# A hybrid decoder step: gate-score levels of both token blocks in one product each, the second block's keys in reversed token order

## The reference, cut to what matters

```
z = forget logits; k_in = (1 - lb) * sigmoid(-z); qh = silu(query logits)
# S_t = diag(f_t) S_{t-1} + k_t^T v_t ;  o_t = S_t^T q_t, so for n >= m
A[n, m] = sum_d q[n, d] k[m, d] exp(b[n, d] - b[m, d])     # b = cumulative sum of log f
o[n]    = sum_m A[n, m] v[m]        S_end = sum_m (k[m] * exp(b_end - b[m]))^T v[m]
```

## Time and profile before

| | |
|---|---|
| median of 3 runs | 1856.31 us |
| the profiled execution's own time | 1854.89 us |
| its span, first to last instruction | 1853.1 us |
| PE busy | 1809.0 us (98%) |
| DVE busy | 1148.3 us (62%) |
| ACT busy | 777.4 us (42%) |
| POOL busy | 278.5 us (15%) |
| mean granted TensorE clock | 0.995 |

### The profile page before, as it was taken

One profiled execution on the slowest core, in us unless ns is written; L12 is line 12 of the kernel. 1 busy time (PEld: TensorE's weight loads), 2 busy tenths in 40 slices (PEclk: granted clock), 3 DMA queues, 4 the chain that ended last, 5 costly groups with the idle time before them and its releaser, 6 DMA issues.

```text
span 1853.1 us, 37457 instructions
## 1 busy us (share of the span) xinstructions
PE 1809.0 (98%) x14672; PEld 1789.6 (97%) x14672; DVE 1148.3 (62%) x1293; ACT 777.4 (42%) x894; POOL 278.5 (15%) x332
## 2 busy tenths in 40 slices
PE   5999999999999999999999999999999999999997
PEld 5999999999999999999999999999999999999996
DVE  8776877768777674555556665555555555545444
ACT  5444444444544453333334344443344334333332
POOL 4441624516235110000000000000000000000001
PEclk9999999999999999999999999999999999999998
DMA  7665646656467555555557655555655555555552
GB/s 230 191 203 171 195 139 194 203 174 195 139 191 209 174 165 178 180 181 177 175 168 229 187 177 181 177 176 178 181 177 176 179 180 176 182 181 179 175 180 102
DMA packets 387002, 333.86 MB, mean 180 GB/s; under 512 B 10240, under 2 KB 385024, under 8 KB 386816
## 3 DMA queue, kind: packets, MB, share of 16 engines
q1 hardware_dynamic: 368000, 318.87, 56.5%
q10 hardware_dynamic: 18944, 14.16, 2.6%
HBM read 316.67 MB, written 16.32 MB: 180 GB/s over the span
## 4 chain that ended last, share of the span: by engine, by line
PE 84%; DVE 6%; issue 3%; DMA 3%; ACT 1%; SPq 1%; POOL 0%; DVEq 0%; ACTq 0%
PE pA L1062 13%; PE pA L1063 13%; PE pA L1064 12%; PE pB L1063 11%; PE pB L1062 11%; PE pB L1064 11%; DMA raw<-in_w_in 3%; PE p L1062 3%; PE p L1063 3%; PE p L1064 3%; DVE lo L703 2%; PE p L1205 1%; DVE hg_scores L914 1%; PE p L1177 1%; SPq L358 1%
## 5 line engine op out<-in xcount | busy, mean ns | idle before, releaser
L703 DVE TENSOR_TENSOR lo<-raw,hi 128x1024 fp32r<-128x1024 f32 x568 | 724.2, 1280 | 575.7 <-ACT hi L407 569.7
L407 ACT CAST hi<-raw 128x1024 fp32r<-128x1024 f32 x568 | 595.6, 1049 | 847.8 <-PE pA L1064 355.9
L1062 PE MATMUL pA<-h_hi,hi 128*128 128x264 f32 x1728 | 500.4, 290 | 19.0 <-DVE lo L703 19.0
L1063 PE MATMUL pA<-h_lo,hi 128*128 128x264 f32 x1728 | 493.9, 286 | 0.0
L1064 PE MATMUL pA<-h_hi,lo 128*128 128x264 f32 x1728 | 493.4, 286 | 0.0
L1062 PE MATMUL pB<-h_hi,hi 128*128 128x264 f32 x1472 | 422.2, 287 | 0.0
L1063 PE MATMUL pB<-h_lo,hi 128*128 128x264 f32 x1472 | 418.8, 285 | 0.0
L1064 PE MATMUL pB<-h_hi,lo 128*128 128x264 f32 x1472 | 418.4, 284 | 0.0
L1062 PEld LDWEIGHTS pA<-h_hi,hi 128*128 128x128 f32 x1728 | 328.1, 190 | 22.7 <-issue 19.2
L1063 PEld LDWEIGHTS pA<-h_lo,hi 128*128 128x128 f32 x1728 | 327.5, 190 | 0.3
L1064 PEld LDWEIGHTS pA<-h_hi,lo 128*128 128x128 f32 x1728 | 327.3, 189 | 0.0
(11 more groups left out here) (250 smaller groups left out, 2486.2 us busy)
## 6 DMA issues: line engine op xcount, KB each, us to landing
raw<-in_w_in SPq DMA_DIRECT2D x224, 512.0 KB, 3.7
raw<-in_w_fin SPq DMA_DIRECT2D x176, 512.0 KB, 3.7
raw<-in_w_fout SPq DMA_DIRECT2D x88, 512.0 KB, 3.5
raw<-in_w_ret SPq DMA_DIRECT2D x32, 512.0 KB, 3.8
raw<-in_w_out SPq DMA_DIRECT2D x32, 512.0 KB, 4.1
S_ret<-in_s_ret SPq DMA_DIRECT2D x8, 1024.0 KB, 8.4
out_ret_s<-S_ret ACTq DMA_DIRECT2D x8, 1024.0 KB, 7.0
raw<-in_w_hg SPq DMA_DIRECT2D x16, 512.0 KB, 3.6
```

Source lines behind the costliest of these rows:

```text
L407: copy(hi[s][:], raw[s][:]).then_inc(hi_done, 1)
L703: tt(lo[s][:], raw[s][:], hi[s][:].bitcast(F32), ALU.subtract).then_inc(split_done, 1)
L1062: mm(outs[t], w_hi, a_hi[:, kt, :], start=(kt == 0), stop=False)
L1063: mm(outs[t], w_hi, a_lo[:, kt, :], start=False, stop=False)
```

## The change

The seven level products of block 1 go away. `k_lev[n]` now has 128 columns: in the lower halves stand block 0's keys as before, and in the columns that were zero stand block 1's keys in reversed token order (reversing the 128 tokens turns lower halves into upper ones). One product then holds, in its 128 rows, keys of both blocks, and the predicate masks pick for block 0's queries the one kind of row and for block 1's the other. All that meets block 1's scores as rows is therefore in reversed order too: the diagonal product takes `hkey_back`, the mask of the diagonal gets a reversed identity, block 1 of `kbar` is written reversed, and the values come from `hval_back`.

Per head it removes 7 products on PE, adds one `tensor_scalar` of 128 columns on DVE (`hkey_back`, step 3), one copy of 128 columns on ACT (`hval_back`, step 15) with a semaphore on which PE waits at step 16, and on POOL it splits 7 writes of `k_lev` and one of `kbar` into two each. At the start, 7 memsets on POOL go away and the constants grow from 3776 to 4352 columns.

```diff
-        k_lev = [alloc(heads, f"k_lev{i}", [P, NP]) for i in range(NLEV)]
+        k_lev = [alloc(heads, f"k_lev{i}", [P, P]) for i in range(NLEV)]
...
                         act.wait_ge(b_free, h * 2 + 3)
+                        copy(hval_back[:], hig[:, 0, P:NP][:, ::-1]).then_inc(hval_turned, 1)
                         fn(hg_sig[:], hig[:, 1, :], ACT.Sigmoid).then_inc(hg_sig_done, 1)
...
-            for i in range(NLEV):
-                nc.gpsimd.memset(k_lev[i][:], 0.0).then_inc(products, 1)
...
                     kl0, _ = halves(k_lev[i][:], s)
+                    kl1, _ = halves(k_lev[i][:, ::-1], s)
+                    n, shape = P // (2 * s), [P, NP // (2 * s), s]
...
-                    step(tt(kl0, k0, g0, ALU.mult))
+                    tt(kl0, k0[:, 0:n], g0[:, 0:n], ALU.mult).then_inc(products, 1)
+                    count[0] += 1
+                    step(tt(kl1, k0[:, n:], g0[:, n:], ALU.mult))
...
-                step(tt(kbar[:], hkey[:, 0:NP], run_g[:], ALU.mult))
+                tt(kbar[:, 0:P], hkey[:, 0:P], run_g[:, 0:P], ALU.mult).then_inc(products, 1)
+                count[0] += 1
+                step(tt(kbar[:, P:NP][:, ::-1], hkey[:, P:NP], run_g[:, P:NP], ALU.mult))
...
                         ts(hkey[:], z_nsig[:], omlb[:, bass.ds(h, 1)], None, ALU.mult).then_inc(forget_done, 1)
+                        ts(hkey_back[:], z_nsig[:, P:NP][:, ::-1], omlb[:, bass.ds(h, 1)], None, ALU.mult)
...
-                            msk = c_level[:, n:n + 1, :].rearrange("p a (b s) -> p a b s", s=s
-                                                                   ).broadcast_to([P, 2, 64 // s, s])
+                            msk = c_level[:, n].rearrange("p k (b s) -> p k b s", s=s)
...
                     pe.wait_ge(parts_done, h * 14 + 14)
-                    natural(p7[:, 0, 0:256], hig[:, 0, :], 128)
+                    pe.wait_ge(hval_turned, h + 1)
+                    natural(p7[:, 0, 0:256], hig[:, 0, :], 128, second=hval_back[:])
...
                     for n in range(NLEV):
-                        mm(p56[:, 0, 64 * n:64 * n + P], k_lev[n][:, 0:P], q_lev[n][:], start=True, stop=True)
-                    for n in reversed(range(NLEV)):
-                        last = mm(p56[:, 1, 64 * n:64 * n + P], k_lev[n][:, P:NP], q_lev[n][:], start=True, stop=True)
+                        last = mm(p56[:, n // 4, (n % 4) * P:(n % 4) * P + P], k_lev[n][:], q_lev[n][:],
+                                  start=True, stop=True)
                     last.then_inc(p56_full, 1)
```

More of the change, by code:

```diff
@@ L86 @@
 K_LEVEL = K_MASK + H * NP
-K_IDENT = K_LEVEL + NLEV * 64
-K_KDEC = K_IDENT + P
+K_IDENT = K_LEVEL + NLEV * P
+K_KDEC = K_IDENT + 2 * P
 K_GAMMA = K_KDEC + 2 * H
@@ L140, in build @@
         hkey = alloc(heads, "hkey", [P, T])
+        hkey_back = alloc(heads, "hkey_back", [P, P])
+        hval_back = alloc(heads, "hval_back", [P, P])
         hquery = alloc(heads, "hquery", [P, T])
@@ L227, in build @@
         c_ident = cst[:, K_IDENT:K_IDENT + P]
-        c_level = cst[:, K_LEVEL:K_LEVEL + NLEV * 64].bitcast(I32).rearrange("p (l j) -> p l j", l=NLEV)
+        c_level = cst[:, K_LEVEL:K_LEVEL + NLEV * P].bitcast(I32).rearrange("p (l b j) -> p l b j", l=NLEV, b=2)
+        c_diag = cst[:, K_IDENT:K_IDENT + 2 * P].rearrange("p (b n) -> p b n", b=2)
         c_kdec = cst[:, K_KDEC:K_KDEC + 2 * H].rearrange("p (b h) -> p b h", b=2)
@@ L271, in build @@
         hg_sig_done = sem("hg_sig_done")
+        hval_turned = sem("hval_turned")
         products = sem("products")
@@ L622, in _ @@
             pool.wait_ge(h_done, 4)
-            for i in range(NLEV):
-                nc.gpsimd.memset(k_lev[i][:], 0.0).then_inc(products, 1)
-            steps = 2 + 4 * NLEV + 4
+            steps = 2 + 5 * NLEV + 5
             def last_outputs(h):
@@ L637, in levels @@
             def levels(h):
-                count = [NLEV]
+                count = [0]
                 def step(ins):
@@ L659, in levels @@
                     kl0, _ = halves(k_lev[i][:], s)
-                    shape = [P, NP // (2 * s), s]
+                    kl1, _ = halves(k_lev[i][:, ::-1], s)
+                    n, shape = P // (2 * s), [P, NP // (2 * s), s]
                     if i:
@@ L670, in levels @@
                 step(tt(run_g[:, 0:P], run_g[:, 0:P], run_f[:, NP - 1:NP].broadcast_to([P, P]), ALU.mult))
-                step(tt(kbar[:], hkey[:, 0:NP], run_g[:], ALU.mult))
-                assert count[0] == NLEV + steps
+                tt(kbar[:, 0:P], hkey[:, 0:P], run_g[:, 0:P], ALU.mult).then_inc(products, 1)
+                count[0] += 1
+                step(tt(kbar[:, P:NP][:, ::-1], hkey[:, P:NP], run_g[:, P:NP], ALU.mult))
+                assert count[0] == steps
             levels(0)
@@ L783, in level_psum @@
             def level_psum(n):
-                return bass.AP(tensor=p56, offset=64 * n, ap=[[2 * 512, P], [512 + 64, 2], [1, 64]])
+                return p56[:, n // 4, (n % 4) * P:(n % 4) * P + P].rearrange("p (k j) -> p k j", k=2)
             def state_lo(out, state, state_hi_part, h, n):
@@ L897, in head @@
                         tt(hg_scores[:, 0:3:2, :], p4[:, 0, 0:256].rearrange("p (b n) -> p b n", b=2),
-                           c_ident.rearrange("p (a n) -> p a n", a=1).broadcast_to([P, 2, P]), ALU.mult
-                           ).then_inc(score_step, 1)
+                           c_diag, ALU.mult).then_inc(score_step, 1)
                         nc.vector.tensor_copy(v_rows[4 * NS:8 * NS, 0:HV], p4[4 * NS:8 * NS, 0, 384:512]
@@ L1077, in _, with natural @@
                 pe.sem_inc(free, 1)
-            steps = 2 + 4 * NLEV + 4
-            def natural(out, src, width):
+            steps = 2 + 5 * NLEV + 5
+            def natural(out, src, width, second=None):
                 for b in range(2):
-                    last = transpose(out[:, b * width:b * width + 128], src[:, b * P:b * P + P], c_ident)
+                    block = src[:, b * P:b * P + P] if second is None or b == 0 else second
+                    last = transpose(out[:, b * width:b * width + 128], block, c_ident)
                 return last
@@ L1158, in attend @@
                 elif i == 16:
-                    pe.wait_ge(products, h * steps + (NLEV + steps))
+                    pe.wait_ge(products, h * steps + steps)
                     pe.wait_ge(p7_free, h * N7 + (TI2 + 1))
                     pe.wait_ge(parts_done, h * 14 + 14)
-                    natural(p7[:, 0, 0:256], hig[:, 0, :], 128)
+                    pe.wait_ge(hval_turned, h + 1)
+                    natural(p7[:, 0, 0:256], hig[:, 0, :], 128, second=hval_back[:])
                     natural(p7[:, 0, 256:512], kbar[:], 128).then_inc(p7_full, 1)
@@ L1167, in attend @@
                     for b in range(2):
-                        mm(p4[:, 0, b * P:b * P + P], hkey[:, b * P:b * P + P], hquery[:, b * P:b * P + P],
-                           start=True, stop=True)
+                        mm(p4[:, 0, b * P:b * P + P], hkey_back[:] if b else hkey[:, 0:P],
+                           hquery[:, b * P:b * P + P], start=True, stop=True)
                     mm(p4[:, 0, 256:384], k_top[:], q_lev[NLEV][:], start=True, stop=True)
@@ L1318, in constants @@
         n_of = (j // s) * 2 * s + s + j % s
-        level.append((m // (2 * s) == n_of // (2 * s)) & (m % (2 * s) < s))
+        seen = (m // (2 * s) == n_of // (2 * s)) & (m % (2 * s) < s)
+        level += [seen, seen[::-1]]
     kdec = gamma[None, None, :] ** (NP - 1 - (np.arange(2)[None, :, None] * P + np.arange(P)[:, None, None]))
@@ L1323, in constants @@
     c[:, K_MASK:K_MASK + H * NP] = mask.transpose(1, 0, 2).reshape(P, H * NP)
-    c[:, K_LEVEL:K_LEVEL + NLEV * 64] = np.concatenate(level, axis=1)
-    c[:, K_IDENT:K_IDENT + P] = np.eye(P)
+    c[:, K_LEVEL:K_LEVEL + NLEV * P] = np.concatenate(level, axis=1)
+    c[:, K_IDENT:K_IDENT + 2 * P] = np.concatenate([np.eye(P), np.eye(P)[::-1]], axis=1)
     c[:, K_KDEC:K_KDEC + 2 * H] = kdec.reshape(P, 2 * H)
```

## The result

The changed kernel takes 1840.72 us (median of 4 runs, 1839.6 to 1842.7) against 1856.38 us for the kernel before (4 runs): ratio 0.9915, 95% interval 0.9898 to 0.9932, so 15.7 us less, between 12.6 and 18.9 us. A second set on another chip gave 0.9917 (0.9904 to 0.9931). Two of the 11 executions of one experiment, x6, fell in a slow state at 2907 and 3537 us and are left out of its median and ratio. The forecast was 1847.5 us with a range down to 1843.8. The direction was right and the time lies outside the range: the gain is nearly twice the 8.8 us forecast, and more than the 12.6 us that the removed products can give, though the interval reaches down to just that.

The account below looks back on a forecast made before the run. PE, busy 98% of the span, was taken as the bound. Removed products gain 10.9 us, hkey_back on DVE costs 2.1, all else 0: 8.8 us less, 1856.3 to 1847.5 us, range 1843.8 to 1852.5.

Parts of the forecast that it names:

- The bound: Whole kernel: PE busy 98% of the span with few waits, so work removed from PE comes off the time.
- the product term: Step 16: PE loses 12.6 us of products; DVE's scores start 1.36 us earlier per head, so 10.9 us gained.
- Cost 0: POOL's 8 more instructions per head: done before PE's step 16, costing nothing to a few tenths in the last head.
- a gain above 12.6 us: Whole kernel: a sign of being wrong, since the removed products can't give more.
- `hkey_back`: DVE at step 3: delays hquery 0.74 us and lo 0.25 us a head, 2.1 us in all; ends -2.8 to +9.1.
- The coupling from step 3 to step 13: DMA chain from lo of chunks 8 and 9 to PE's step-13 wait moves along, so lo's whole delay counts, 1.5 us.
- rival B: DVE at step 3: hkey_back costs little or nothing; 1845.4 us, at best 1843; chance 0.14.
- Masks: DVE's seven predicated copies, 2.82 us: same elements, other strides, taken as 0; ends 5.6 us less or more.
- `hval_back`: ACT copy at step 15: 0.3 us, covered, cost 0; without the cover up to 0.2 us a head.
- constants: Start: 576 more columns, 1.6 us of DMA once, hidden behind ACT's 6.25 us wait for PE.
- POOL as the bound: Step 16: slow reversed POOL writes make PE wait for products; slower above 8.2 us added work per head; chance 0.04.
- rival E: Step 16: slower kernel, PE waiting for POOL's reversed writes, 1912 us if each took 1.9 us more; chance 0.04.

Follow-up runs that it names:

- x6: Kernel before, with only POOL's k_lev writes of levels 4 to 6 and its kbar write split in two: 1853.35 us, ratio 0.9987.
- x11: Changed kernel with DVE's five small sample instructions moved from step 3 to step 5 and its 7 level products issued twice: 1847.86 us, ratio 0.9952.
- x8: Changed kernel with DVE's five small instructions on the sample's keys and queries moved from step 3 to step 5: 1836.67 us, ratio 0.9898.
- x2: Kernel before, with POOL's 7 k_lev writes and the kbar write each split in two, not reversed, still 14 level products: 1853.26 us, ratio 0.9981.
- x5: Kernel before, with only POOL's k_lev write of level 0 split in two: 1855.07 us, ratio 0.9995.
- x1: Kernel before, plus DVE writing hkey_back between hkey and hquery, which nothing reads: 1855.53 us, ratio 0.9992.
- x10: Kernel before, with DVE's five small sample instructions moved from step 3 to step 5: 1848.27 us, ratio 0.9952.
- x7: Changed kernel with DVE's work on the scores of step 16 put in front of lo of chunk 20: 1840.85 us, ratio 0.9926.
- x12: Changed kernel again, unedited, on another chip: 1841.81 us, ratio 0.9917.
- x9: Changed kernel with the five small sample instructions moved to step 5 and the step 16 scores put before lo of chunk 20: 1835.34 us, ratio 0.9880.
- x3: Changed kernel with hkey_back made by DVE at step 13 from hkey instead of at step 3: 1842.55 us, ratio 0.9924.

## Why the prediction was wrong

**The bound and the product term: right.** PE was the bound, 8 x 1.58 us of its work went, and DVE took part of it back through step 17. Forecast 10.9 us; measured 10.2 us between step 13 and 17 and 10.4 us in the traces of x11 and x8. The 0.6 us too much is the semaphore step in front of L912: I took 0.03 us from another pair of instructions, and it took 0.11 us.

**The step that failed** is the one on POOL: "POOL runs longer beside DVE's step 11, where the wait of step 13 is made; it ran there before as well, so I add nothing", and with it "Cost 0" for the split. I asked only whether POOL would be done in time (it is: `kbar` of head 7 ends at 595.39 us, PE's step 16 begins at 601.30) and not what the size of POOL's instructions does to DVE, although I had just used that blocking for `hquery`. A blocked DVE instruction waited for the end of one POOL instruction, so halving POOL's instructions shortened what DVE waited for (`hq_only` 0.50 to 0.33 us, a `v_parts` instruction 0.38 to 0.24 us). x2 shows it alone: 3.5 us (1.9 to 5.2) gained; x5 and x6 show its two places. In sum, the stretch from step 17 to step 13 was forecast 2.1 us longer and came out 3.8 us shorter. Part of that is luck: between 1.8 and 2.6 us of it hang on a race that the prediction did not know of. The prediction's own sign of being wrong, a gain above 12.6 us, came true.

**`hkey_back`: the local picture right, the sum too high.** 0.72 us later for `hquery` (0.74), POOL waiting for it in turn, no slack behind it. But the 2.1 us assumed head 0's 1.89 us from `hquery` to `lo`; it was 1.24 or 1.72 us, by the race and by the half-size write. With the race lost and the write whole it is the 1.89 us assumed, and the 0.25 us a head worked out from it came out as 0.23 (x1, heads 2 to 6). Head 1, for which I took 0.6 us, lost 0.2 (34.07 for 33.88 us). Alone (x1) it moved step 13 back by 0.14 us a head, 1.0 us in all, and its time did not differ from the kernel before.

**The coupling from step 3 to step 13: right, and more than I made of it.** That the DMA chain moves with `lo` of chunks 8 and 9 was in the working as a reason to pass a cost on. x10 shows that it was worth 8.3 us in the kernel before. Since I had the wait of 5.9 us, the rival in which it shrinks deserved a price; rival B allowed only that `hkey_back` be free. A forecast with both terms as measured, 10.2 + 3.8 = 14.0 us, would have lain at 1842.4 us.

**Masks, `hval_back`, constants, POOL as the bound: right at zero.** Masks 2.82 us before and after; no wait of PE at step 16; rival E did not come.

**Still open.** Why POOL's copy of `run_f` wins the race against DVE's cast in 16 of 19 heads while the write of level 0 behind it is whole (before heads 2 to 7, x1 heads 2 to 7, x6 all seven), and in only 22 of 49 while that write is split (after, x2 to x5, x7, x12), was not settled: both instructions start before that write, within 0.01 us. Heads of one execution are not independent, so even that splitting makes the race easier to win is only likely. Nor could the spread of the landing of chunk 14 be tied to anything: `hi` of chunk 14 starts 11.2 to 13.0 us behind the issue of `S_ret` in the 98 heads of the fourteen traces.

## What to carry to other kernels

Where two engines hold each other back, the price of an instruction is what it makes the other one wait, so its length counts and not only its sum: splitting an instruction on the engine with time to spare can speed up the one without. Before pricing an edit, follow every wait of the bound engine back to its source; a wait of 1 us a head on a DMA went back, over a load queue, to five tiny instructions ten steps earlier, and moving them (8.3 us) was worth nearly as much as removing half of the level products (about 10 us). And a gain above what the removed work can give is a sign that some other wait moved; adding up the stretches between two fixed points of each iteration finds it.

## What the runs showed of the hardware that I had not expected

A `tensor_scalar` with a reversed source of 128 columns was blocked by POOL: 1.36 us beside `ret_o`, 0.28 us with POOL idle. POOL's writes in reversed order were no slower than the forward ones: in head 7 either half of `kbar` took 0.46 us. The means of `k_lev` hold much waiting: the first, forward halves took 0.75 us in the mean and 0.37 in the median, the second, reversed ones 0.51 and 0.32 us, where the whole ones took 0.77 us in the mean:

```profile
L668 POOL TENSOR_TENSOR k_lev<-hkey,run_g 128x64 f32<-128x64 f32 x56 | 41.8, 746 | 0.6
...
L670 POOL TENSOR_TENSOR k_lev<-hkey,run_g 128x64 f32<-128x64 f32 x56 | 28.3, 505 | 0.0
```

A race of 0.01 us between two engines' instructions decided 0.5 us in a head. The kernel before spread over 1854.0 to 1859.6 us in 27 runs, while the kernels with the parts moved spread over 1.3 us in 4 runs (x8), 1.6 us in 5 (x10), 1.9 us in 5 (x11) and 2.9 us in 4 (x9). More runs also spread further, so this does not show the race to be the source of the spread. Another source is in the traces. In eight of the fourteen (x1, x2, x3, x5, x8 to x11) the granted clock fell to 0.5 (1.2 GHz) for 3.4 us between 1689 and 1715 us. It fell 0.6 to 1.3 us after PE had gone back to work from an idle stretch of 2.3 to 2.8 us; in the other six PE sat idle for 2.2 to 2.6 us at the same place and its clock stayed up. The part behind step 17 of head 7 took 1232.3 to 1232.8 us in these eight and 1230.5 to 1231.1 us in the other six.
